# A decoder step on one core: one stretch of 17 cleared products at the start, half of the transposed x copied by another engine, and head norms by four column groups

## The reference, cut to what matters

```python
def _rmsnorm(x, g):
    xf = x.astype(jnp.float32)
    y = xf * lax.rsqrt(jnp.mean(xf * xf, axis=-1, keepdims=True) + EPS)
    return (y * g.astype(jnp.float32)).astype(x.dtype)
...
    h = _rmsnorm(x, g_pre_mix) * (1.0 + sc1) + sh1
...
    o = _rmsnorm(o, g_norm).reshape(B, L, W_A) * jax.nn.silu(ag.astype(f32))
...
    o_b = (_rmsnorm(o_b, g_subln) * (1.0 - lam_init)).reshape(B, L, W_B).astype(h.dtype)
    merged = jax.nn.sigmoid(gate_a) * (o_a @ w_proj_a) + jax.nn.sigmoid(gate_b) * (o_b @ w_proj_b)
```

## Time and profile before

| What | Value |
|---|---|
| Median of three runs | 1261.01 us (1259.24 to 1261.58) |
| Span of the profiled execution, first to last instruction | 1258.5 us |
| What lies around the span, taken as median minus span | 2.5 us |
| PE, DVE, ACT busy, share of the span | 88%, 47%, 18% |
| Mean DMA rate over the span | 386 GB/s |
| Chain of work that ended last | DMA 45%, PE 27%, DVE 1% |

### The profile page before, as it was taken

One profiled execution on the slowest core, in us unless ns is written; L12 is line 12 of the kernel. 1 busy time (PEld: TensorE's weight loads), 2 busy tenths in 40 slices (PEclk: granted clock), 3 DMA queues, 4 the chain that ended last, 5 costly groups with the idle time before them and its releaser, 6 DMA issues.

```text
span 1258.5 us, 23992 instructions
## 1 busy us (share of the span) xinstructions
PE 1102.0 (88%) x9856; PEld 456.6 (36%) x9856; DVE 588.2 (47%) x1166; ACT 230.7 (18%) x420; POOL 68.5 (5%) x126
## 2 busy tenths in 40 slices
PE   8999999999988697996887979999966995667996
PEld 4776777785322131321222322333211331112332
DVE  3536744444654252563353544666532552332654
ACT  3002510141311110220111211112100211100212
POOL 0312020250100000000000000000000000000000
PEclk9999999999989897998798999999988998888999
DMA  9979994599899999999999999999999999999995
GB/s 342 312 245 347 317 339 154 187 384 366 284 428 429 426 429 426 429 425 429 426 428 428 428 426 393 409 424 427 428 427 428 427 426 430 424 431 425 428 428 236
DMA packets 67619, 485.30 MB, mean 386 GB/s; under 512 B 6421, under 2 KB 29450, under 8 KB 40762
## 3 DMA queue, kind: packets, MB, share of 16 engines
q1 hardware_dynamic: 59312, 461.07, 88.9%
q0 software_dynamic: 7104, 19.65, 4.9%
q10 hardware_dynamic: 1130, 3.51, 0.8%
HBM read 479.47 MB, written 4.72 MB: 385 GB/s over the span
## 4 chain that ended last, share of the span: by engine, by line
DMA 45%; PE 27%; DVE 1%; issue 0%; DVEq 0%; ACT 0%; ACTq 0%
DMA big<-in_w_down 26%; PE PB L1247 13%; DMA big<-in_w_gate_up 13%; PE PB L1274 7%; DMA hTG<-in_w_down 5%; PE PB L1214 2%; PE PB L1201 2%; PE PB L1206 1%; PE PB L1229 1%; PE PB L1221 1%; PE PB L1240 0%; PE PB L1186 0%; PE PB L1232 0%; DVE big L1623 0%; DVE big L1620 0%
## 5 line engine op out<-in xcount | busy, mean ns | idle before, releaser
L1247 PE MATMUL PB<-big,cst 128*32 128x512 f32 x2768 | 355.0, 657 | 109.2 <-DMA big<-in_w_gate_up 109.2
L2189 DVE TENSOR_TENSOR tok<-PB,cst 32x512 f32<-32x512 f32 x188 | 129.1, 687 | 261.7 <-ACT cst L1554 259.8
L1247 PEld LDWEIGHTS PB<-big,cst 128*32 128x32 f32 x2768 | 89.0, 115 | 345.2 <-issue 181.1
L1274 PE MATMUL PB<-big,cst 128*32 128x512 f32 x1408 | 166.6, 602 | 12.8 <-DMA big<-in_w_down 12.7
L2165 DVE TENSOR_SCALAR mod<-PB 64x256 f32<-64x256 f32 x96 | 41.0, 427 | 209.1 <-PE PB L1247 208.4
L756 PE MATMUL PB<-hTG,big 128*128 128x264 f32 x576 | 136.5, 391 | 0.4 <-DVE hTG L1617 0.4
L756 PEld LDWEIGHTS PB<-hTG,big 128*128 128x128 f32 x576 | 106.9, 190 | 27.3 <-issue 10.8
L1544 ACT ACTIVATE mod<-PB 64x256 f32<-64x256 f32 x96 | 36.1, 376 | 422.3 <-PE PB L1247 421.7
L1274 PEld LDWEIGHTS PB<-big,cst 128*32 128x32 f32 x1408 | 39.2, 110 | 96.8 <-issue 65.8
L1201 PE MATMUL PB<-wide,att 128*32 128x256 f32 x784 | 57.9, 415 | 5.1 <-DVE att L2159 4.9
L1554 ACT ACTIVATE cst<-PB 128x512 f32<-128x512 f32 x48 | 28.7, 597 | 178.2 <-PE PB L1274 178.2
(11 more groups left out here) (378 smaller groups left out, 970.9 us busy)
## 6 DMA issues: line engine op xcount, KB each, us to landing
big<-in_w_gate_up SPq DMA_DIRECT2D x115, 2048.0 KB, 31.0
big<-in_w_down SPq DMA_DIRECT2D x57, 2048.0 KB, 23.9
hTG<-in_w_gate_up SPq DMA_DIRECT2D x13, 2048.0 KB, 37.1
big<-in_w_mod SPq DMA_DIRECT2D x24, 1024.0 KB, 7.5
big<-in_w_in SPq DMA_DIRECT2D x22, 1024.0 KB, 9.2
hTG<-in_w_down SPq DMA_DIRECT2D x6, 2048.0 KB, 24.0
wide<-in_cache_k POOLq DMA_DIRECT2D x16, 256.0 KB, 6.8
big<-in_w_out SPq DMA_DIRECT2D x4, 1024.0 KB, 10.5
```

The lines of the kernel that those rows point to most:

```text
L1247: mm = pe.matmul(GU[32 * j:32 * j + 32, :], mo["xT"][:, (2 * u + r) * M:(2 * u + r + 1) * M], groups(w[:, r * 2 * D:(r + 1) * 2 * D])[:, j ...
L1274: mm = pe.matmul(DN[32 * j:32 * j + 32, :], mo["actT"][:, (4 * u + r) * M:(4 * u + r + 1) * M], w[:, r * D + half * 512:r * D + (half + 1) ...
L2189: mm = dve.tensor_tensor(mo["y"][rows, :], DN[rows, :], mo["y_part"][other, :], ALU.add)
```

## The change

Three edits. (1) At the start, the cleared products are regrouped: 17 instead of 6 ahead of `vt`, 5 instead of 4 behind it, 2 instead of 7 ahead of the first `scale_part`. (2) ACT copies only xt0, xt2, xt4, xt6 to `hT`; DVE copies the others. (3) `head_sums` makes four products of 264 columns, one per head, into four groups of 32 output partitions of one bank (nb or na). ACT takes logarithm (with scale and eps) and exponential over 264 columns, all heads at once (`head_roots`). PE sends each head's roots back to 128 partitions (`head_back`: 32 rows of weights that pick one row, one bank per head, nb0 to nb3 or na0 to na3), and DVE multiplies out of PSUM (`head_norm`). DVE's `head_sum` and `ms_ready` are gone; the second half of w_proj_a waits for PE's sums.

```diff
-    ... oa2 oa3 ou20 ou30 ou21 ou31 nb0 nb1 nb2 mt2 so
-    na0 na1 na2""".split()
+    ... oa2 oa3 ou20 ou30 ou21 ou31 nb mt2 nb0 nb1 nb2 nb3 so
+    na na0 na1 na2 na3""".split()
...
-                sp.wait_ge(S("ms_ready"), 1)
+                sp.wait_ge(S("aux_full"), AUX["nb"] + 1)
...
-            idle_products(6)
+            idle_products(17)
...
             def head_sums(branch, sq):
 
-                for i in range(3):
-                    bank = begin(f"n{branch}{i}")
-                    pe.wait_ge(S(f"sq{branch}_ready"), 1)
-                    full(pe.matmul(bank[:, 0:352], C("ones"), sq[:, i * 352:(i + 1) * 352], start=True, stop=True))
+                bank = begin(f"n{branch}")
+                pe.wait_ge(S(f"sq{branch}_ready"), 1)
+                for h in range(H):
+                    mm = pe.matmul(bank[32 * h:32 * h + 32, 0:T], C("ones")[:, 0:32], sq[:, h * T:(h + 1) * T],
+                                   start=True, stop=True)
+                full(mm)
+
+            def head_back(branch, roots, *heads):
+
+                banks = [begin(f"n{branch}{h}") for h in heads]
+                pe.wait_ge(S("hrms_ready"), 1 if branch == "b" else 2)
+                for h, bank in zip(heads, banks):
+                    rows = slice(32 * h, 32 * h + 32)
+                    mm = pe.matmul(bank[:, 0:T], C("onehot_e")[rows, 0:1].to_broadcast([32, P]), roots[rows, 0:T],
+                                   start=True, stop=True, tile_position=(32 * h, 0))
+                    full(mm)
...
-            idle_products(4)
+            idle_products(5)
             scale_bias()
-            idle_products(7)
+            idle_products(2)
...
-            in_T(10, [(outer, 1, 1)], [(head_sums, "b", KDf), (mod_cols, "mt2", 2)], [(out_sample, 2), (out_sample, 3)],
+            in_T(10, [(outer, 1, 1)], [(head_sums, "b", KDf), (mod_cols, "mt2", 2)], [(out_sample, 2), (head_back, "b", GCf, 0, 1, 2), (out_sample, 3),
+                  (head_back, "b", GCf, 3)],
...
-            for k in range(KC):
+            for k in range(0, KC, 2):
                 act.wait_ge(S("aux_full"), AUX[f"xt{k}"] + 1)
...
+            def head_roots(branch, roots):
+
+                act.wait_ge(S("aux_full"), AUX[f"n{branch}"] + 1)
+                act.wait_ge(S("aux_free"), AUX[f"n{branch}"])
+                do(act.activation(roots[:, 0:T], aux(f"n{branch}")[:, 0:T], ACT.Ln, scale=1.0 / DV, bias=eps[:, :]))
+                act.nop().then_inc(S("aux_free"), 1)
+                do(act.activation(roots[:, 0:T], roots[:, 0:T], ACT.Exp, scale=-0.5), "hrms_ready")
...
+            for k in range(1, KC, 2):
+                copy(hT[:, k, :], bank(f"xt{k}")[:, 0:T])
+                dve.wait_ge(S("aux_free"), AUX[f"xt{k}"])
+                dve.nop().then_inc(S("aux_free"), 1)
...
+            def head_norm(branch, OT, *heads):
+
+                for h in heads:
+                    roots = bank(f"n{branch}{h}")[:, 0:T]
+                    if branch == "a":
+                        tt(OT[:, h, :], OT[:, h, :], roots, ALU.mult)
+                    else:
+                        stt(OT[:, h, :], OT[:, h, :], sv("gsl"), roots, ALU.mult, ALU.mult)
                     free()
```

More of the change, by code:

```diff
@@ L132 @@
     pt0 pt1 pt2 pt3 ob0 ob1 ss ob2 ob3 kt0 kt1 pd as0 as1
-    kv0 vas kv1 kks kv2 ou00 ou10 kv3 mt1 ou01 ou11 oa0 oa1 sv oa2 oa3 ou20 ou30 ou21 ou31 nb0 nb1 nb2 mt2 so
-    na0 na1 na2""".split()
+    kv0 vas kv1 kks kv2 ou00 ou10 kv3 mt1 ou01 ou11 oa0 oa1 sv oa2 oa3 ou20 ou30 ou21 ou31 nb mt2 nb0 nb1 nb2 nb3 so
+    na na0 na1 na2 na3""".split()
 AUX_ORDER += "lp sm0 lc sm1 xs rt2 xa0 xa1 l0 rt0 xb0 xb1 l1 rt1".split()
@@ L1034, in branch @@
                         head_sums("a", ETf)
+                    if first + s == 5:
+                        head_back("a", RAf, 0, 1, 2)
+                    if first + s == 6:
+                        head_back("a", RAf, 3)
                     if name == "pb":
@@ L1446, in _ @@
                 if j == 6:
-                    act.wait_ge(S("ms_ready"), 1)
-                    do(act.activation(GCf, GCf, ACT.Ln, bias=eps[:, :]))
-                    do(act.activation(GCf, GCf, ACT.Exp, scale=-0.5), "hrms_ready")
+                    head_roots("b", GCf)
                 take(gbT, "gb", j, ACT.Sigmoid)
@@ L1452, in _ @@
             do(act.activation(ETf, OAf, ACT.Square), "sqa_ready")
[L1453 to L1459, removed]
+            head_roots("a", RAf)
             def y_square(c, i):
@@ L1916, in sample_states @@
                         dve.nop().then_inc(S("s0_ready"), 1)
[L1918 to L1921, removed]
-                    free()
[L1923 to L1933, removed]
+            def head_norm(branch, OT, *heads):
[5 more added lines that the diff above has]
+                        stt(OT[:, h, :], OT[:, h, :], sv("gsl"), roots, ALU.mult, ALU.mult)
+                    free()
+                if 3 in heads:
+                    dve.nop().then_inc(S("oF_ready"), 1)
             dve.wait_ge(S("v_used"), 2)
@@ L1963, in _ @@
             sample_states(1, 1)
-            head_sum("b", GCf)
             shift_cols(A2, bank("mt2"), 0)
@@ L1967, in _ @@
             tt(wrA[:, :, :], wr[:, :, :], A2[:, :, 0:1].to_broadcast([P, KC, E]), ALU.mult)
+            head_norm("b", OB, 0, 1, 2)
             dve.wait_ge(S("osa_used"), H)
             copy(vals, PB[4][:, :], "vals_ready")
-            head_norm("b", OB, GC, GCf)
+            head_norm("b", OB, 3)
             b = bank("so")
@@ L1982, in _ @@
             dve.nop().then_inc(S("oa_gated"), 1)
[L1983 to L1987, removed]
+            for s in range(4):
+                merge_b(s)
+            head_norm("a", OA, 0, 1, 2)
+            merge_b(4)
+            head_norm("a", OA, 3)
+            for s in range(5, KC):
                 merge_b(s)
```

## The result

The changed kernel takes 1265.64 us, median of 22 runs (1260.85 to 1271.06), against 1260.76 us (1259.15 to 1266.41) for the kernel before, also 22 runs. The ratio is 1.0029 with a 95% interval of 1.0018 to 1.0041: slower, by 4.9 us between the medians and by 3.7 us between the means (1265.19 and 1261.53 us). Forecast was 1260.3 us, with 0.07 on slower. The profiled execution took 1266.4 us; its span is 1264.7 us against 1258.5. The 2.5 us in the table of times before mixed a median with the span of a faster execution: by 1.7 us, the profiled one of before took about 1260.2 us.

What follows compares the result with a forecast made beforehand. PE's work before 340 us was taken to set the end, with the DMA-bound expert stream moving along. Front -0.9, branch b -0.5 and branch a +0.7 made -0.7: 1260.3 us against 1261.0; eight in ten 1258.0 to 1262.8.

Steps and rivals of the forecast that it cites:

- 0.07 on slower: Whole kernel: chance that the change is slower by more than 0.2% (2.5 us).
- At the raised clock it ends at 13.64 + 1.07 = 14.7: Start: second scale part begins at 13.64 us when its weights land and takes 1.07 us; PE then waits for xn.
- -0.9 us at the start of the first projection: Start: first input projection begins at 23.85 us instead of 24.77, a gain of 0.9 us.
- The level falls back: Start, chance 0.15: PE loses its clock level waiting between scale parts; front 0, heads +0.2, 1261.2 us.
- `vt` at 7.50 us: Start: `vt` begins near 7.8 us, behind 17 cleared products whose clock rises after about two thirds.
- The shift of the start reaches the end nearly one to one: Before 340 us: a microsecond gained or lost on PE moves the end by one, unless a transfer intervenes.
- In branch b the mechanism: Branch b: overlapped head sums, ACT waiting for DVE's bank, roots slightly late for PE, overlapped returns; -0.5 us in all.
- the 0.82 us wait: Branch b's sums: PE's old wait for DVE to free a sample bank, 0.82 us, goes from PE.
- the fourth return: Branch b, ahead of gb7: needs the bank DVE frees with its first product at 252.65 us, then takes 0.55.
- Branch a: Branch a: sums 0.77 and returns 0.84 twice replace 1.77 us of old sums; roots hidden; +0.7 us.
- the switch: Head sums and returns: changing between product shapes on PE costs 0.15 to 0.3 us each time.
- A transfer between 25 and 340 us: Between start and expert stream: the forecast is wrong if a transfer there swallows or enlarges the shift.

Runs made afterwards that it cites:

- The filled waits: Changed kernel with five instead of two cleared products ahead of the first scale part and six between the first two: 1260.94 us, ratio 0.9997 to before.
- the profile with the first one filled: Changed kernel with five instead of two cleared products ahead of the first scale part, nothing added between the first two: 1261.81 us, ratio 0.9995 to before.

## Why the prediction was wrong, point by point

**The step that failed** is "At the raised clock it ends at 13.64 + 1.07 = 14.7". I let the level rise at two thirds of the 17 products, which it did, and then took it as kept through the waits of 0.90 and 1.49 us for weight pieces. In the profiled run it fell to 0.50 between 13.0 and 13.2 us, the second scale part took 1.94 us instead of 1.07, and the level stayed low to 30 us; by the times, most runs (18 of 22) go that way. From there the sum goes the other way. Against the earlier trace rows: the second scale part starts 0.15 us earlier, the first four groups 3.35 for 2.70, the second four 3.35 for 2.16, two scale parts 1.94 for 1.07, together +3.4 us at the end of the last scale part; another 0.7 in the transposes and cleared products behind it and 0.5 in the first projection. Forecast was -0.9 us at the start of the first projection; measured +4.12 there and +4.66 behind it. The Trainium skill, "TensorE: Matmul & The Clock Gate", HAM oscillation — how this bites in real kernels, tells of a kernel whose clock drops again in each wait of about 3 to 5 us for a transfer between short bursts of products. The filled waits agree in kind; the wait in which the level fell here was 1.49 us, shorter than any in that case, and over the same wait the profile with the first one filled kept it.

**The rival was seen and mis-priced.** "The level falls back" had chance 0.15, with the sentence "the transposes cost what they did". They did not: in the profile of before the level rises at about the first transposed groups and stays. That price could have been worked out from the earlier trace rows: the rows from the first groups on, each at up to twice its time. I priced the fall against the slow rows of the old start and forgot that the fast ones were at stake too.

**A table of one execution.** The profile of before is one draw, and a low one; the runs above 1263.5 us show that the old start has another outcome. Nothing in the three times shown (1259.24 to 1261.58) told so.

**What held.** `vt` at 7.50 us (forecast 7.8), in part by luck, since in the five profiles with 17 products these took between 5.79 and 7.09 us; from its start to the end of ACT's small root 2.6 us (2.77). The shift of the start reaches the end nearly one to one. In branch b the mechanism held to the wait: sums 0.59 (0.65), the 0.82 us wait gone from PE, ACT waiting for DVE instead, PE waiting 0.45 us for the roots (0.35), three returns 0.65 (0.65). From the sums to gb7 it gave 0.31 (7.86 us against 8.17) instead of 0.5: logarithm and exponential took 0.48 and 0.42 instead of 0.39, the first half of `out_sample` with its switch 0.64 instead of 0.55, and the fourth return 0.64 instead of 0.55. Another 0.09 went in the tile ahead of the sums (3.75 us to their start, before 3.66), which leaves the 0.22.

**Branch a** came out at +0.69 (+0.7), by other terms: sums 0.58 (0.77), returns 0.65 and 0.63 (0.84 each), but the branch's own products beside them are slower, 5.54 us for the three tiles behind the sums and 1.98 for the tile that stands alone, where four products take 1.79 in a row of tiles. I read this as the switch, paid in the neighbours: 0.17 to 0.2 us each. All these rows make +0.46; another 0.09 lies between gb7 and the sums and 0.14 in the ten tiles behind, neither followed, so that the total met the forecast is luck. The Trainium skill's rule of a drain at a change of tiling mode ("TensorEngine Tiling (Array Packing)", Key Properties) agrees with the slower neighbours, though no run isolates a switch. The Trainium skill's drain of 1.38 us beside a table load ("ScalarE: Activation LUTs", What ACT_TABLE_LOAD costs) does not show on either side: the load ends at 252.99 + 1.28 = 254.27 us and the logarithm starts at 254.29; that ends at 254.77, and the next load starts at 254.87.

**A transfer between 25 and 340 us** did add 0.85 us in the profiled run (the cache load), as I had named among the things to make me wrong; by the other profiles (6.2 to 7.6 us from its issue to landing, with no order by kernel) it belongs to the execution, not to the change.

## What to carry to other kernels

A stretch of empty work that raises PE's clock pays only if the level is still up when the work that it is meant for starts: list the waits between the two, try filling them, and judge by many runs. When a clock level is part of a sum, price both levels for every row behind the point where it may fall, those that ran fast in the trace included. And if a kernel's single runs fall into groups, look for the outcome that differs between them before taking one profile as the kernel's time.

## What was not expected of the hardware

PE stayed at half clock through 10.2 us in which it was busy for 9.81 (window 13.1 to 23.3 us above), on short transposes and 32-column scale parts; it came back behind cleared products and the first full 128x264 products. In the profile of before it rose within the same transposes (2.70, then 2.16 us), so this work alone does not hold it down. With the old groups, the second scale part took 1.94 us in one profile and 1.07 in another, and the runs of one kernel fall into the same groups of times: I take it that the level differs between executions of one kernel, though each kernel has only one profile. What decides it in a single execution stays open. And the clock column cannot be trusted by itself: the window of the changed kernel reads 1.00 from 0 to 6 us, where eleven cleared products last 4.87 us, 0.44 us each against 0.25 for the five behind `vt`. In the changed kernel with the old groups it reads 1.00 from 13 to 30 us too, though scale parts take 1.94 us there; the durations tell the level.
